# The first mixer as one stage: unscaled input split, two convolution chunks on VectorE, output projection in two passes

## The reference, cut to what matters

```python
def hybrid_mixer(n, w_in, ..., w_out):            # n = rms_norm(x, mix_norm_g)
    z = einsum("bsd,de->bse", n, w_in)            # 1024 -> 2048
    x_lru, g_lru, a_glu, b_glu = split(z)         # 512 channels each
    xc = depthwise_conv(x_lru, lru_conv_w, ...)   # 4 taps
    h_fwd, h_bwd = rg_lru(xc, ..., False), rg_lru(xc, ..., True)
    y_lru = (h_fwd + h_bwd) * gelu(g_lru)
    c = depthwise_conv(a_glu * sigmoid(b_glu), conf_conv_w, ...)   # 31 taps
    y_conv = silu(group_layer_norm(c, ...))       # groups of 64 channels
    y = concatenate([rms_norm(y_lru, beta_lru), rms_norm(y_conv, beta_conv)])
    return einsum("bse,ed->bsd", y, w_out)        # added to x

def rg_lru(x, ...):       # per way: r, i = sigmoid(block_diag_linear(x)), then
    log_a = 8 * r * log_sigmoid(lam); a = exp(log_a)
    u = sqrt(-expm1(2 * log_a)) * (i * x)
    h[t] = a[t] * h[t-1] + u[t]
```

## Time and profile before

| | us |
|---|---|
| median of 3 runs | 4152.44 (4151.73 to 4155.09) |
| the profiled execution | 4152.22 |
| its span | 4150.4 |
| TensorE busy | 3699.8 (89%) |
| VectorE busy | 2133.0 (51%) |
| ScalarE busy | 1503.1 (36%) |
| POOL busy | 1962.8 (47%) |
| mean granted TensorE clock | 0.936 |

### The profile page before, as it was taken

How to read it: one execution, slowest core, us unless ns; L and a number is a source line. 1 busy time by engine, 2 the same in 40 slices (tenths; PEclk the granted TensorE clock), 3 DMA queues, 4 the chain that set the end, 5 groups by cost and what they waited for, 6 DMA issues and landing times. The chain is left out here.

```text
span 4150.4 us, 50844 instructions
## 1 busy us (share of the span) xinstructions
PE 3699.8 (89%) x17284; PEld 3086.9 (74%) x17284; DVE 2133.0 (51%) x3337; ACT 1503.1 (36%) x2617; POOL 1962.8 (47%) x1517
## 2 busy tenths in 40 slices
PE   6948999988999999999979857999979997569999
PEld 5526998988999999888868425788768885247887
DVE  4663498865999776733234244333243321644330
ACT  3322455753333343534223213433234421333432
POOL 4724576436788787555414102444435543004444
PEclk9978999999999999999989767999989998689999
DMA  3002354558999899333323001233323335002332
GB/s 116 20 15 83 111 172 146 202 215 337 371 404 403 333 352 354 106 96 96 96 90 96 26 0 37 90 92 94 89 64 96 95 93 129 0 7 90 96 92 90
DMA packets 172780, 570.20 MB, mean 137 GB/s; under 512 B 15457, under 2 KB 58593, under 8 KB 155140
## 3 DMA queue, kind: packets, MB, share of 16 engines
q1 hardware_dynamic: 152244, 427.68, 31.3%
q0 software_dynamic: 20432, 141.31, 9.1%
HBM read 518.85 MB, written 50.07 MB: 137 GB/s over the span
## 5 line engine op out<-in xcount | busy, mean ns | idle before, releaser
L267 POOL TENSOR_TENSOR weight_low<-weight_ring,weight_high 128x512 fp32r<-128x512 f32 x1264 | 1719.9, 1383 | 1801.4 <-ACT weight_high L239 1312.0
L281 PE MATMUL banks<-normed_high,weight_high 128*128 128x512 f32 (+1 forms) x2592 | 974.4, 376 | 86.3 <-PEq L390 43.9
L282 PE MATMUL banks<-normed_low,weight_high 128*128 128x512 f32 (+1 forms) x2592 | 966.1, 373 | 0.0
L239 ACT ACTIVATE weight_high<-weight_ring 128x512 fp32r<-128x512 f32 x632 | 398.9, 631 | 1330.1 <-PE banks L288 1226.7
L281 PEld LDWEIGHTS banks<-normed_high,weight_high 128*128 128x128 f32 x2592 | 497.1, 192 | 161.8 <-issue 78.5
L288 PE MATMUL banks<-normed_high,weight_low 128*128 128x512 f32 (+1 forms) x2592 | 589.0, 368 | 6.3 <-POOL weight_low L267 6.0
L282 PEld LDWEIGHTS banks<-normed_low,weight_high 128*128 128x128 f32 x2592 | 496.3, 191 | 64.4 <-issue 1.6
L288 PEld LDWEIGHTS banks<-normed_high,weight_low 128*128 128x128 f32 x2592 | 473.6, 188 | 71.2 <-POOL weight_low L267 9.8
L241 ACT ACTIVATE weight_high<-weight_ring 128x512 fp32r<-128x512 f32 (+1 forms) x632 | 389.3, 616 | 79.0 <-PE banks L288 77.9
L281 PE MATMUL banks<-parked_high,weight_high 128*128 128x384 f32 x768 | 262.0, 341 | 15.0 <-ACT weight_high L239 9.5
L1739 DVE TENSOR_TENSOR square<-square,banks 128x512 f32<-128x512 f32 x88 | 60.5, 687 | 416.5 <-PE banks L288 414.9
(11 more groups left out here) (362 smaller groups left out, 5661.3 us busy)
## 6 DMA issues: line engine op xcount, KB each, us to landing
weight_ring<-in_experts SPq DMA_DIRECT2D x256, 512.0 KB
weight_ring<-in_ffn_gate SPq DMA_DIRECT2D x88, 512.0 KB
weight_ring<-in_ffn_up SPq DMA_DIRECT2D x88, 512.0 KB
weight_ring<-in_ffn_down SPq DMA_DIRECT2D x64, 512.0 KB
expert_gates<-spread_space SPq DMA_DIRECT2D x6, 4096.0 KB, 12.2
parked_space<-expert_gates SPq DMA_DIRECT2D x24, 768.0 KB
parked_space<-parked_activations SPq DMA_DIRECT2D x24, 768.0 KB
weight_ring<-in_a_w_in SPq DMA_DIRECT2D x28, 512.0 KB
```

The lines of the kernel that those rows point to most:

```text
L239: m.nc.scalar.activation(m.w_hi[:, s % PARTS, 0:HALF], m.ring[:, s, 0:HALF], ACT.Copy).then_inc(m.half_high, 1)
L267: m.nc.gpsimd.tensor_tensor(m.w_lo[:, s % PARTS, at], m.ring[:, s, at], m.w_hi[:, s % PARTS, at].bitcast(FP), ALU.subtract).then_inc(done, 1)
L281: m.nc.tensor.matmul(out, w_hi, hi(c), start=(first and c == 0), stop=False)
L282: m.nc.tensor.matmul(out, w_hi, lo(c), start=False, stop=False)
```

## The change

- `start`: SP issues the vectors first, one piece of x, the first panel, the rest of x, panel 1, and only then the constants, panels 2 and 3. VectorE's squares and ScalarE's first split move into the mixer.
- The input is no longer normalised: x times the gain is split into high and low part, and each of the 16 panels is multiplied by the row norm when VectorE evacuates it. TensorE makes the row sum after panel 1. The panels come in the order of `HYBRID_ORDER`: a and b of chunks 2, 3, 0, 1, then x, then g. Sigmoid and gelu are applied by ScalarE behind VectorE's scaling.
- VectorE does two chunks (2 and 3) of the long convolution, three taps for each panel from panel 4 on, between its evacuations; TensorE has 62 taps instead of 93.
- The recurrence's decay is an Exp on ScalarE; the 1 + tanh and its reciprocal go.
- Group norm, both row norms and the output projection stand in the same block, interleaved by hand. `w_out` is laid out in eight panels of two half panels: four for the lru branch, four for the convolution branch (`half_panel`), so each output chunk gets two sums, each scaled by its branch's row norm at its evacuation (`add_out`) and added to the residual.

```diff
+HYBRID_ORDER = [(kind, c) for c in (2, 3, 0, 1) for kind in ("glu", "sigmoid")] + \
+               [(kind, c) for kind in ("x", "gelu") for c in range(LRU_C4)]
...
@@ -339,22 +342,18 @@
     with nc.Block() as block:
         @block.sync
         def _(sp):
-            sp.dma_start(m.const[:, :], io["constants"]).then_inc(loaded, 16)
+            sp.sem_inc(m.low, SLOTS)
+            sp.sem_inc(m.half_low, SLOTS)
             sp.dma_start(m.vec[:, :], io["vectors"]).then_inc(loaded, 16)
             for k in range(4):
                 sp.dma_start(m.x[:, 2 * k:2 * k + 2, :], io["x"][:, 2 * k:2 * k + 2, :]).then_inc(x_loaded[k], 16)
-            sp.sem_inc(m.low, SLOTS)
-            sp.sem_inc(m.half_low, SLOTS)
+                if k == 0:
+                    load_panel(m, sp, 0, 0, *ahead[0])
             for s, (source, width) in enumerate(ahead):
+                if s:
+                    load_panel(m, sp, s, s, source, width)
+                if s == 1:
+                    sp.dma_start(m.const[:, :], io["constants"]).then_inc(loaded, 16)
...
+def half_panel(m, pe, p, s, banks, chunks):
+    half = HALF // P
+    ready = ((m.half_high, m.half_low), (m.high, m.low))
+    for k in range(2):
+        out = m.bank[banks[k]][:, :]
+        high, low = ready[k]
+        pe.wait_ge(high, p + 1)
+        for c in range(half):
+            w_hi = m.w_hi[:, s % PARTS, (k * half + c) * P:(k * half + c + 1) * P]
+            m.nc.tensor.matmul(out, w_hi, m.n_hi[:, chunks + c, :], start=(c == 0), stop=False)
+            m.nc.tensor.matmul(out, w_hi, m.n_lo[:, chunks + c, :], start=False, stop=False)
+        pe.wait_ge(low, low_count(p))
+        for c in range(half):
+            w_lo = m.w_lo[:, s % PARTS, (k * half + c) * P:(k * half + c + 1) * P]
+            ins = m.nc.tensor.matmul(out, w_lo, m.n_hi[:, chunks + c, :], start=False, stop=(c == half - 1))
+        ins.then_inc(m.used if k else m.half_used, 1)
...
+            weight_panels(m, sp, io["w_in"], IN, panels_ahead(io["w_out"]))
+            m.panels += IN
+            weight_panels(m, sp, io["w_out"], OUT, ahead)
+            m.panels -= IN
...
+            for j in range(IN):
+                s = j % SLOTS
+                pe.wait_ge(m.bank_free[s], fill0 + j // SLOTS + 1)
+                ready = (lambda c: pe.wait_ge(x_low, c + 1)) if j == 0 else None
+                part_products(m, pe, low_count(first + j), m.bank[s][:, :], s, DC, *own_input(m), True, True, ready)\
+                    .then_inc(m.used, 1)
+                if j == 1:
+                    pe.wait_ge(loaded, 32)
+                    pe.wait_ge(prepared.sem, prepared.base + 1)
+                    scale.sums(pe)
...
+            def out_panel(k):
+                banks = [2 * k % SLOTS, 2 * k % SLOTS + 1]
+                for b in banks:
+                    pe.wait_ge(m.bank_free[b], out_fill0 + 2 * k // SLOTS + 1)
+                if k in (0, OUT // 2):
+                    pe.wait_ge(out_low, k + C4 if k else C4)
+                half_panel(m, pe, out_first + k, k % SLOTS, banks, 0 if k < OUT // 2 else C4)
+            gates()
+            average(2)
+            average(3)
+            taps(0, CONF_TAPS // 2)
+            square_sum(2)
+            square_sum(3)
+            taps(CONF_TAPS // 2, CONF_TAPS + CONF_TAPS // 2)
+            average(0)
+            taps(CONF_TAPS + CONF_TAPS // 2, PE_TAPS)
+            square_sum(0)
+            row_sum(0, lru_sq)
+            average(1)
+            out_panel(0)
+            square_sum(1)
+            for k in range(1, OUT // 2):
+                out_panel(k)
+            row_sum(1, sq)
+            for k in range(OUT // 2, OUT):
+                out_panel(k)
...
+            act.wait_ge(loaded, 32)
+            for c in range(DC):
+                if c % 2 == 0:
+                    act.wait_ge(x_loaded[c // 2], 16)
+                nc.scalar.activation(m.n_hi[:, c, :], m.x[:, c, :], ACT.Copy, scale=V("mix_g", c)).then_inc(x_high, 1)
+                if c == 1:
+                    split_high(m, act, (0, 0), 0)
+            shapes = 0
+            for j in range(IN):
+                kind, c = HYBRID_ORDER[j]
+                split_next(m, act, first // SLOTS + j // SLOTS, j % SLOTS)
+                if j == 1:
+                    scale.root(act)
+                    order.step(act, nc.scalar.activation(lam[:, 0, :], m.vec[:, VEC["lam"]:VEC["lam"] + 8], ACT.Abs))
+                    nc.scalar.activation(lam[:, 1, :], lam[:, 0, :], ACT.Exp, scale=-1.0).then_inc(x_high, 1)
+                if kind in ("gelu", "sigmoid"):
+                    dst, func = (g_gelu, ACT.Gelu_apprx_tanh) if kind == "gelu" else (conv, ACT.Sigmoid)
+                    shapes += 1
+                    act.wait_ge(scaled, shapes)
+                    nc.scalar.activation(dst[:, c, :], dst[:, c, :], func).then_inc(shaped, 1)
...
+            def lru_input(c):
+                act.wait_ge(lru_ready, c + 1)
+                nc.scalar.activation(m.n_hi[:, c, :], lru[:, c, :], ACT.Copy, scale=V("beta_lru", c)).then_inc(out_high, 1)
+                nc.scalar.activation(lru_sq[:, c, :], lru[:, c, :], ACT.Square).then_inc(branch_squared, 1)
...
+            square_centred(2)
+            square_centred(3)
+            act.wait_ge(prepared.sem, prepared.base + 2)
+            act.wait_ge(gate_evac, 4 * C4)
+            for w in ways:
+                ins = nc.scalar.activation(decay[:, w, :], root[:, w, :], ACT.Exp, scale=lam[:, 6, w:w + 1])
+            order.step(act, ins)
+            for w in ways:
+                ins = nc.scalar.activation(root[:, w, :], root[:, w, :], ACT.Tanh, scale=lam[:, 7, w:w + 1])
+            order.step(act, ins)
+            for w in ways:
+                nc.scalar.activation(root[:, w, :], root[:, w, :], ACT.Sqrt).then_inc(root_done, 1)
+            root_of(2)
+            root_of(3)
+            split_next(m, act, out_first // SLOTS, 0)
+            lru_input(0)
+            evacuate(0)
+            lru_input(1)
+            square_centred(0)
+            lru_input(2)
+            lru_input(3)
+            root_of(0)
+            evacuate(1)
+            square_centred(1)
+            row_root(0)
+            root_of(1)
+            split_next(m, act, out_first // SLOTS, 1)
+            for c in gln[:-1]:
+                conv_input(c)
+            split_next(m, act, out_first // SLOTS, 2)
+            conv_input(gln[-1])
+            for c in gln:
+                conv_square(c)
+            split_next(m, act, out_first // SLOTS, 3)
+            split_next(m, act, out_first // SLOTS + 1, 0)
+            row_root(1)
+            for k in range(5, OUT):
+                split_next(m, act, out_first // SLOTS + 1, k % SLOTS)
...
+            dve.wait_ge(loaded, 32)
+            for c in range(DC):
+                dve.wait_ge(x_high, c + 1)
+                vec.scalar_tensor_tensor(out=m.n_lo[:, c, :], in0=m.x[:, c, :], scalar=V("mix_g", c),
+                                         in1=m.n_hi[:, c, :].bitcast(FP), op0=ALU.mult, op1=ALU.subtract)\
+                   .then_inc(x_low, 1)
+            for c in range(DC):
+                add_squares(m, dve, c)
+            dve.sem_inc(prepared.sem, 1)
...
+            scale.inverse(dve)
...
+            def long_conv(a, b):
+                for tap in range(a, min(b, CONF_TAPS)):
+                    for c in DVE_CONV:
+                        src, w = glu_pad[:, c, tap:tap + T], V("conf_w", c * CONF_TAPS + tap)
+                        if tap == 0:
+                            ins = vec.tensor_scalar(conv[:, c, :], src, w, V("conf_b", c), ALU.mult, ALU.add)
+                        else:
+                            ins = vec.scalar_tensor_tensor(out=conv[:, c, :], in0=src, scalar=w, in1=conv[:, c, :],
+                                                           op0=ALU.mult, op1=ALU.add)
+                    order.step(dve, ins)
+                    if tap == CONF_TAPS - 1:
+                        dve.sem_inc(glu_ready, 1)
+            TAPS = 3
+            for j in range(IN):
+                kind, c = HYBRID_ORDER[j]
+                dst = {"glu": glu_pad[:, c, CONF_LEFT:CONF_LEFT + T], "sigmoid": conv[:, c, :],
+                       "x": x_pad[:, c, LRU_LEFT:LRU_LEFT + T], "gelu": g_gelu[:, c, :]}[kind]
+                dve.wait_ge(m.used, used_count(first + j))
+                order.step(dve, vec.tensor_tensor(dst, m.bank[j % 4][:, :], m.sum[:, :], ALU.mult))
+                dve.sem_inc(m.bank_free[j % 4], 1)
+                if kind in ("sigmoid", "gelu"):
+                    dve.sem_inc(scaled, 1)
+                if kind == "x":
+                    short_conv(c)
+                if j == 2:
+                    lambdas()
+                if j >= 4:
+                    if j <= 10 and j % 2 == 0:
+                        if j == 4:
+                            gated(0)
+                            gated(1)
+                        elif j <= 8:
```

(60 more changed lines are left out.)

338 lines of the change are left out of this document (165 added, 173 removed).

## The result

The changed kernel takes 4097.27 us in the median of 4 runs (4090.62 to 4110.44) beside 4153.76 (4151.73 to 4155.65) for the kernel before: a ratio of 0.9868 with a 95% interval of 0.9841 to 0.9895. Four more runs on another chip gave 4094.06 (4090.05 to 4097.63) beside 4155.12: 0.9858 [0.9843, 0.9874]. Predicted were 4087 and a range of 4066 to 4112.

What follows compares the result with a forecast made beforehand. The end of the mixer's last sum of squares was taken to decide, with limits differing by stage: 53 + 86 + 31 + 108 = 278 us instead of 343.2, 65 less than 4152.2, so 4087, range 4066 to 4112.

Steps and rivals of the forecast that it cites:

- the 3805 us behind it: Everything after the mixer's last sum of squares: runs as before; a change by more than 3 us would refute the prediction.
- eight ways: Recurrences on VectorE after the first root: eight times 2 x 0.75 + 1.28 and 0.1 of order, given as 23.2 us.
- Start: From the kernel's beginning to the first long-convolution tap, behind panel 4: 53 us, with TensorE starting at about 15.7.
- VectorE through the input projection: From 53 to 139 us: VectorE's list of 70.4 us plus 15.4 of GpSimd collisions, 0.7 for each of 22 instructions.
- TensorE's hole ahead of panel 14: In the input projection: TensorE idles some 18 us before panel 14, restarts slowly, and still ends before VectorE.
- no lock: Rival: collisions with GpSimd cost VectorE nothing, its part falls by 15.4 and 8.4 us, total 4063; chance 0.13.
- full blocking: Rival: every GpSimd instruction stops VectorE for 1.29 us, 20 us more, total 4107; chance 0.13.
- The rival by which TensorE and ScalarE starve: Waits ahead of panels lower TensorE's clock; six panels at 7.2 us instead of 5.45, total 4096; chance 0.14.
- Gates to the first root: From 139 to 170 us: gates 14.1, averages, centring and squares 3.3, ScalarE's Exp, Tanh and root 13.3; taken as 31.
- VectorE to the end: From 170 to 278 us: VectorE's list 95.2, collisions 8.4 and waits 4.4, together 108 us.
- the largest single term: In VectorE's list after the first root: the eight reciprocals of 1 + tanh, 26.8 us, are gone.

Runs made afterwards that it cites:

- Runs 1 and 2: The changed kernel and the kernel before, both unchanged, timed and profiled again: 4094.06 us and 4156.87 us.
- run 3: Changed kernel with GpSimd filling the low parts of all sixteen w_in panels by memset instead of subtraction: 4067.42 us.
- Run 9: Changed kernel with the recurrence's decay as before, by Tanh and VectorE's reciprocal of 1 + tanh instead of Exp: 4116.34 us.
- run 4: Changed kernel with two taps behind each panel instead of three, the other 7 behind those of panel 15: 4084.31 us, 0.9838 of the kernel before.
- run 8: Run 7's kernel with one tap a panel, twenty behind the last evacuation, squares and averages of chunks 2 and 3 moved later: 4070.80 us.
- run 7: Changed kernel with a semaphore of their own for the constants, so the input split waits for vectors and x alone: 4094.32 us.

## Why the prediction was right, step by step

**The bound and the part behind.** "When the last sum of squares of the mixer ends" decides, and it did: 61.8 us less against 65 forecast. "If the 3805 us behind it change by more than 3" I called myself wrong, and in the profiled execution they changed by 20.1. Runs 1 and 2 show it isn't the change (3811.2 and 3810.5), but the bound of 3 was too tight: the same part took 3807.2 and 3810.5 in two executions of the same kernel. Of the 10 us between 4087 and 4097.27, 3 are the mixer's; no profile shows the median execution, but the rest isn't in the mixer, whose gain repeats within 1.3 us.

The total is better than its terms. The first two stretches took 7.4 us longer than forecast (4.6 and 2.8), the last two 4.0 less (1.0 and 3.0), which leaves 3.4; that they offset one another is luck. One term is added up wrongly: eight ways at 2 x 0.75 + 1.28 + 0.1 are 23.0, not 23.2, and nothing hangs on it.

**Start, 53 forecast, 57.6 measured.** The split at 13.7 came at 14.0 and TensorE at 15.7 at 16.0. The low parts ended at 24.3, not 21, and the squares at 37.1, not 33.4. The low parts were priced without collisions; they have them:

```profile
...
L884 DVE SCALAR_TENSOR_TENSOR normed_low<-residual,vectors,normed_high x8: 737/840/1761, 14.9 to 22.6; 128x512 fp32r<-128x512 f32 x8
...
```

```profile
...
L887 DVE SCALAR_TENSOR_TENSOR normed_low<-residual,vectors,normed_high x8: 743/746/752, 14.7 to 20.2; 128x512 fp32r<-128x512 f32 x8
...
```

The first row is after, the second run 3 (the same line; median 0.746 us, no tail). Their excess is (7.31 - 4.06) = 3.3 us by the two timelines, nearly all of the squares' 3.7. From there to panel 4 it took 20.5 us where 19.6 were forecast. So the step was right and its term undersized by 4.6, of which 3.3 is the very effect that was priced one step later.

**VectorE through the input projection, 86 forecast, 88.8 measured.** Of this, 15.9 are collisions (15.4 forecast) by the length of the stretch in run 3, 17.9 by VectorE's busy time there. Both rivals on the price fell: no lock would leave out 15.9, full blocking at 1.29 an instruction would add 13 (22 x 0.59). TensorE's hole ahead of panel 14 was 18.1 us (18 forecast). The remainder, 2.3, was not traced. The rival by which TensorE and ScalarE starve needs a word, because its 4096 lies nearer to the measured 4097.27 than the forecast does. TensorE's hole and its slow restart are there (granted clock 0.88 in this stretch), but from 57.7 to 281.4 the only waits of VectorE for TensorE are the 14.6 us for the gates, so they did not reach the end; what brings the time near 4096 is the part behind.

**Gates to the first root, 31 forecast, 30.0 measured.** The gates took 14.4 (14.1), what VectorE does ahead of Exp 2.2 instead of 3.3. One table load stands ahead of Exp and one ahead of the root, and none between Exp and Tanh. ScalarE's timeline there:

```profile
...
163.01 1.28 ACT L842 ACT_TABLE_LOAD   x1
164.31 5.01 ACT L842 ACTIVATE hybrid_space<-hybrid_space 128x512 f32<-128x512 f32 x8
169.35 5.00 ACT L845 ACTIVATE hybrid_space<-hybrid_space 128x512 f32<-128x512 f32 x8
174.37 1.28 ACT L848 ACT_TABLE_LOAD   x1
...
```

**VectorE to the end, 108 forecast, 105.0 measured.** VectorE was busy for 98.0 of it, so the list was the bound, as said: 98.0 instead of the 103.6 of list and collisions, and 7.0 of waits instead of 4.4. Run 9 confirms the largest single term, the reciprocals that went: 3.35 us each, eight times, in VectorE's list and nearly all on the path. That its net 26.3 is close to the 26.8 of the earlier trace rows is chance, as other terms of 7.7 and 6.6 us stand against each other in it.

**Where the gain comes from.** Undone one at a time, the edits are worth 26 us (decay by Exp), 11 (first pass beside the second branch's norm), 8 (early first panel) and 7 (second chunk on VectorE), 52 of 61. They aren't independent and were not undone together, so the sum is no proof; the remaining 9 would be the late row norms and the block's missing barrier, neither of which was tried alone.

**What the prediction missed.** It took the order of VectorE's list as given. That list ran the taps ahead of the evacuations, while the same engine idled 14.4 us behind them for the gates; run 4 has nine taps there and its mixer ends 15.7 us earlier (1.8 of it from the start), run 8 has twenty (and some squares) for 18 (276.3 - 258.1). It took the shared semaphore for a fixed cost of the start, where run 7 got 6 us back.

## What to carry to other kernels

Write down the limiting engine's list by stretch, and place its movable work in its own waits: twenty taps of each chunk, with some squares, cost 18 us less behind the last evacuation than between the evacuations. Where VectorE instructions with two SBUF inputs run beside GpSimd work that reads SBUF, add a surcharge for every GpSimd instruction (0.72 us here on average, 0.98 in a dense run), at the start of the kernel too. Give an operand that is needed first a semaphore of its own.

## What the runs showed of the hardware that was not expected

A collision costs both sides: VectorE's taps go from a median of 0.752 to at most 1.780 us, GpSimd's subtractions from a minimum of 1.289 to a median of 1.692, and the price on VectorE's list is 0.72 us for each GpSimd instruction on average and 0.98 in a dense run, neither 0 nor the full 1.29. A GpSimd memset beside the same taps cost nothing that shows (0.862 at most). Exp and Tanh followed one another without a table load (169.35 is 0.03 us behind the end of 164.31 + 5.01), where Sqrt needed 1.28; "ScalarE: Activation LUTs" of the Trainium skill (Table sets) puts exp and tanh into one set, and the trace agrees. The part behind the mixer, the same instructions in every kernel here, took between 3806 and 3827 us in the executions that were profiled, so a single execution is uncertain by some 0.2% here, and once by 0.5%.
